# Four changes at once in a feed-forward layer by a seven-product scheme: other PSUM banks for the turned gates, down products with the weights' remainders last, one weight sum moved from a transfer to VectorE, and a new order on three engines

## The reference

```
def swiglu(x, wg, wu, wd):
    return (jax.nn.silu(x @ wg) * (x @ wu)) @ wd

h = rms_norm(x, g_ffn_pre[i])
gu = h @ w_gate_up[i]
f = (jax.nn.silu(gu[..., :D_FF]) * gu[..., D_FF:]) @ w_down[i]
x = x + rms_norm(f, g_ffn_post[i])
```

## Time and profile before

| | us |
|---|---|
| median of 3 runs | 1564.68 |
| lowest and highest | 1564.57, 1565.01 |
| the profiled execution | 1565.01 |
| its span in the profile | 1563.2 |
| TensorE matmuls busy in it | 1540.2 |
| VectorE busy | 1314.4 |
| ScalarE busy | 1019.2 |
| GpSimd busy | 155.2 |

### The profile page before, as it was taken

How to read it: one execution, slowest core, us unless ns; L and a number is a source line. 1 busy time by engine, 2 the same in 40 slices (tenths; PEclk the granted TensorE clock), 3 DMA queues, 4 the chain that set the end, 5 groups by cost and what they waited for, 6 DMA issues and landing times.

```text
span 1563.2 us, 20989 instructions
## 1 busy us (share of the span) xinstructions
PE 1540.2 (99%) x8060; PEld 1257.7 (80%) x8060; DVE 1314.4 (84%) x1420; ACT 1019.2 (65%) x1400; POOL 155.2 (10%) x232
## 2 busy tenths in 40 slices
PE   9999999999999999999999999999999999999998
PEld 8778878877888888888877888888878887788886
DVE  6869998787999989998658699988999766789996
ACT  7756776675676666666558467665766556656674
POOL 1001000040100010002030000000000203000000
PEclk9999999999999999999999999999999999999999
DMA  8338887623978868899540488977798652077992
GB/s 294 135 107 257 229 258 240 202 82 111 303 219 243 268 203 241 255 291 246 178 135 2 148 237 240 292 209 263 216 278 259 202 187 82 1 269 214 281 261 79
DMA packets 154611, 321.17 MB, mean 205 GB/s; under 512 B 5736, under 2 KB 50016, under 8 KB 151440
## 3 DMA queue, kind: packets, MB, share of 16 engines
q1 hardware_dynamic: 135408, 261.87, 48.3%
q0 software_dynamic: 18672, 57.42, 18.8%
q10 hardware_dynamic: 432, 0.53, 0.1%
HBM read 293.59 MB, written 1.05 MB: 188 GB/s over the span
## 4 chain that ended last, share of the span: by engine, by line
PE 86%; DVE 7%; DMA 3%; ACT 3%; issue 1%; SPq 0%; POOL 0%; POOLq 0%; DVEq 0%; ACTq 0%
PE pair L2893 9%; PE pair L2894 9%; PE pair L2897 9%; PE bank L2680 8%; PE bank L2682 7%; PE bank L2681 7%; PE pair L2804 7%; PE bank L2774 6%; PE pair L2808 4%; PE bank L2747 3%; PE pair L3168 2%; PE bank L3219 1%; DVE w_lo L1688 1%; PE bank L3189 1%; PE pair L2951 1%
## 5 line engine op out<-in xcount | busy, mean ns | idle before, releaser
L1052 ACT ACTIVATE w_hi<-raw 128x2048 fp32r<-128x2048 f32 (+2 forms) x171 | 325.0, 1904 | 155.9 <-DVE raw L1855 52.3
L1688 DVE TENSOR_TENSOR w_lo<-raw,w_hi 128x2048 fp32r<-128x2048 f32 (+2 forms) x167 | 378.9, 2273 | 51.0 <-ACT w_hi L1052 50.4
L1688 DVE TENSOR_TENSOR w_lo<-fold_raw,w_hi 128x2048 fp32r<-128x2048 f32 x144 | 329.4, 2288 | 28.7 <-ACT w_hi L1052 26.3
L1052 ACT ACTIVATE w_hi<-fold_raw 128x2048 fp32r<-128x2048 f32 x144 | 275.9, 1916 | 80.9 <-PE bank L2682 32.6
L2680 PE MATMUL bank<-w_hi,hid_hi 128*128 128x512 f32 x528 | 206.8, 392 | 0.3 <-DVE hid_lo L1814 0.2
L2682 PE MATMUL bank<-w_lo,hid_hi 128*128 128x512 f32 x528 | 205.8, 390 | 0.0
L2681 PE MATMUL bank<-w_hi,hid_lo 128*128 128x512 f32 x528 | 205.6, 389 | 0.0
L2893 PE MATMUL pair<-w_hi,xs_hi 128*128 128x512 f32 x384 | 154.2, 401 | 0.0
L2894 PE MATMUL pair<-w_hi,xs_lo 128*128 128x512 f32 x384 | 150.3, 391 | 0.0
L2804 PE MATMUL pair<-xt,w_hi 128*128 128x512 f32 x528 | 129.0, 394 | 0.1
L2893 PE MATMUL pair<-w_hi,xt 128*128 128x512 f32 x288 | 115.5, 401 | 1.1 <-DVE hid_lo L1915 1.1
(11 more groups left out here) (356 smaller groups left out, 2676.2 us busy)
## 6 DMA issues: line engine op xcount, KB each, us to landing
raw<-in_ffn_wd SPq DMA_DIRECT2D x44, 1024.0 KB, 9.2
fold_raw<-in_w_gate_up SPq DMA_DIRECT2D x32, 1024.0 KB, 7.5
fold_raw<-in_ffn_wg SPq DMA_DIRECT2D x32, 1024.0 KB, 6.5
fold_raw<-in_ffn_wu SPq DMA_DIRECT2D x32, 1024.0 KB, 7.3
fold_raw<-fold_raw POOLq DMA_DIRECT2D x24, 1024.0 KB, 7.2
raw<-in_w_down SPq DMA_DIRECT2D x22, 1024.0 KB, 8.5
raw<-in_w_in SPq DMA_DIRECT2D x21, 1024.0 KB, 6.3
fold_raw<-in_ffn_wu POOLq DMA_DIRECT2D x16, 1024.0 KB, 11.2
```

The lines of the kernel that those rows point to most:

```text
L1052: act.activation(w_hi[u % RING][:, 0:filled(u)], raw_of(u)[:, 0:filled(u)], ACT.Copy)\
L1688: dve.tensor_tensor(w_lo[s][:, 0:filled(u)], raw_of(u)[:, 0:filled(u)], w_hi[s][:, 0:filled(u)].bitcast(F32), ALU.subtract)\
```

## The change

- `turn_fold` writes banks 2 and 3. `fold_hidden` and `fold_rest` read there. The waits of the products follow: first and second wait for the readers of banks 0 and 1, fifth for `fold_rest(k, 0)`, fourth for `fold_rest(k, 1)`. TensorE takes first and second ahead of fifth.
- `down_inner` (groups 1 to 7, and 9 but in FFN 1) and `down_half` issue all rounded-by-rounded matmuls of their places, then all with the hidden values' remainder, then all with the weights' remainder, and wait for `hidden_lo` and `lo_ready` only ahead of the second and the third set.
- `add_to_lower` goes. VectorE makes the sum (`four_sum`), and `SUM_STEP` counts it as a VectorE step.
- The unit numbers of a fold, and the lists of SP, ScalarE and VectorE get a new order.

```diff
 FOLD_AT = ((7, 8, 9, 10, 11, 12, 14),
-           (17, 18, 16, 19, 20, 21, 23),
-           (26, 27, 25, 28, 29, 30, 32),
-           (35, 36, 34, 37, 38, 39, 41))
+           (16, 17, 18, 19, 20, 21, 23),
+           (25, 26, 27, 28, 29, 30, 32),
+           (34, 35, 36, 37, 38, 39, 41))
-SUM_STEP = (1, 16, 1, 16)
+SUM_STEP = (1, 16, 1, 1)
...
 SP
                 load_right(0)
+                load_down(2)
                 load_down(1)
-                load_down(2)
...
+                load_down(3)
                 load_down(4)
-                load_down(3)
+                load_left(2)
                 load_upper(2)
-                load_left(2)
...
                 load_left(3)
+                load_lower(3)
                 load_right(3)
-                load_lower(3)
...
 GpSimd
-                pool.wait_ge(fold_made[THREE_SUM], fold_index(f, k) + 1)
-                pool.wait_ge(lo_ready, ffns[f][0] + FOLD_AT[k][1] + 1)
-                pool.dma_start(quarters(LOWER), quarters(LEFT), accum_op=ALU.add)\
-                    .then_inc(fold_made[FOUR_SUM], 16)
...
 ScalarE
-                    act.activation(hid_hi[g % 2][:, :], bank[b], ACT.Copy).then_inc(hidden_hi, 1)
+                    act.activation(hid_hi[g % 2][:, :], bank[2 + b], ACT.Copy).then_inc(hidden_hi, 1)
...
+                first_out(1)
+                quarter_rounded(1, 4)
                 fifth_out(1)
-                quarter_rounded(1, 4)
-                first_out(1)
                 sum_rounded(1, 5)
+                second_out(1)
                 down_rounded(3)
-                second_out(1)
                 sum_rounded(1, 6)
...
 VectorE
+                def four_sum(k):
+                    landed(k, LOWER)
+                    dve.wait_ge(fold_made[THREE_SUM], fold_index(f, k) + 1)
+                    dve.wait_ge(lo_ready, u0 + FOLD_AT[k][1] + 1)
+                    dve.tensor_tensor(fold_raw[LOWER][:, :], fold_raw[LEFT][:, :], fold_raw[LOWER][:, :], ALU.add)\
+                       .then_inc(fold_made[FOUR_SUM], 1)
...
```

```diff
 TensorE
                 def first_product(k):
...
-                        pe.wait_ge(hidden_lo, hidden_base + FOLD_GROUPS[k - 1][0] + 1)
+                        pe.wait_ge(third_copied, fold_index(f, k))
...
                 def second_product(k):
-                        pe.wait_ge(hidden_lo, hidden_base + FOLD_GROUPS[k - 1][1] + 1)
+                        pe.wait_ge(fold_gate[0], fold_index(f, k))
...
                 def fifth_product(k):
...
-                        pe.wait_ge(fold_up[0], fold_index(f, k))
-                        pe.wait_ge(fold_gate[1], fold_index(f, k))
+                        pe.wait_ge(hidden_lo, hidden_base + FOLD_GROUPS[k - 1][0] + 1)
...
                 def fourth_product(k):
+                        pe.wait_ge(hidden_lo, hidden_base + FOLD_GROUPS[k - 1][1] + 1)
...
+                def down_terms(u, g, places):
+                    pe.wait_ge(hi_ready, u + 1)
+                    pe.wait_ge(hidden_hi, hidden_base + g + 1)
+                    for m, t, b in places:
+                        pe.matmul(ACC[2 * t + b][:, :], hid_hi[p][:, SEQ * m + P * t:SEQ * m + P * (t + 1)],
+                                  w_hi[s][:, D * m + 512 * b:D * m + 512 * (b + 1)], start=False, stop=False)
+                    pe.wait_ge(hidden_lo, hidden_base + g + 1)
+                    for m, t, b in places:
...
+                    pe.wait_ge(lo_ready, u + 1)
+                    for m, t, b in places:
...
+                def down_inner(g):
+                    down_terms(u0 + DOWN_AT[g], g, [(m, t, b) for m in range(2) for t in range(NT) for b in range(2)])\
+                        .then_inc(unit_used, 1)
...
                 turn_fold(0)
-                fifth_product(1)
                 first_product(1)
                 second_product(1)
+                fifth_product(1)
                 sixth_product(1)
                 third_product(1)
                 seventh_product(1)
-                down(3)
+                down_inner(3)
                 fourth_product(1)
-                down(4)
+                down_inner(4)
                 turn_fold(1)
...
                 if f == 1:
                     down_quarters(((u0 + DOWN_AT[9], 9, 1), (u0 + DOWN_AT[10], 10, 0)), ("ffn1", 0))
                 else:
-                    down(9)
+                    down_inner(9)
                     down(10)
```

More of the change, by code:

```diff
@@ L1914, in fold_rest @@
                     dve.wait_ge(hidden_hi, hidden_base + g + 1)
[L1915 removed]
+                    dve.tensor_tensor(hid_lo[g % 2][:, :], bank[2 + b], hid_hi[g % 2][:, :].bitcast(F32), ALU.subtract)\
                        .then_inc(hidden_lo, 1)
@@ L1920, in ffn @@
                 add_cross(0)
+                row_sums()
                 split_lo(u0 + GATE_AT[1])
@@ L1973, in ffn @@
                 split_lo(u0 + FOLD_AT[1][6])
+                fold_multiply(1, 0)
                 split_lo(u0 + DOWN_AT[4])
                 upper_sum(2)
+                second_gate(1)
                 second_up(1)
-                fold_multiply(1, 0)
-                second_gate(1)
-                split_lo(u0 + FOLD_AT[2][2])
-                fold_multiply(1, 1)
-                split_lo(u0 + FOLD_AT[2][0])
-                three_sum(2)
-                fold_rest(1, 0)
-                split_lo(u0 + FOLD_AT[2][1])
-                fold_rest(1, 1)
+                split_lo(u0 + FOLD_AT[2][0])
+                fold_multiply(1, 1)
+                split_lo(u0 + FOLD_AT[2][1])
+                fold_rest(1, 0)
+                three_sum(2)
+                split_lo(u0 + FOLD_AT[2][2])
                 split_lo(u0 + FOLD_AT[2][3])
@@ L2950, in turn_fold @@
                             first = SEQ * (j % 2) + P * t
-                            last = pe.transpose(bank[j // 2][:, first:first + P], hid[t][:, P * j:P * (j + 1)], ident)
+                            last = pe.transpose(bank[2 + j // 2][:, first:first + P], hid[t][:, P * j:P * (j + 1)], ident)
                     last.then_inc(fold_turned, 1)
@@ L2957, in down_half @@
                     s = u % RING
-                    if half == 0:
-                        pe.wait_ge(lo_ready, u + 1)
-                        pe.wait_ge(hidden_lo, hidden_base + g + 1)
-                    for t in range(NT):
-                        for m in range(2):
-                            lo = SEQ * m + P * t
-                            last = three(ACC[2 * t + half][:, :], hid_hi[p][:, lo:lo + P],
-                                         hid_lo[p][:, lo:lo + P],
-                                         w_hi[s][:, D * m + 512 * half:D * m + 512 * (half + 1)],
-                                         w_lo[s][:, D * m + 512 * half:D * m + 512 * (half + 1)], False, False)
+                    last = down_terms(u, g, [(m, t, half) for m in range(2) for t in range(NT)])
                     if half:
                         last.then_inc(unit_used, 1)
+                def down_terms(u, g, places):
+                    s, p = u % RING, g % 2
+                    pe.wait_ge(hi_ready, u + 1)
[5 more added lines that the diff above has]
+                    for m, t, b in places:
+                        pe.matmul(ACC[2 * t + b][:, :], hid_lo[p][:, SEQ * m + P * t:SEQ * m + P * (t + 1)],
+                                  w_hi[s][:, D * m + 512 * b:D * m + 512 * (b + 1)], start=False, stop=False)
+                    pe.wait_ge(lo_ready, u + 1)
+                    for m, t, b in places:
+                        last = pe.matmul(ACC[2 * t + b][:, :], hid_hi[p][:, SEQ * m + P * t:SEQ * m + P * (t + 1)],
+                                         w_lo[s][:, D * m + 512 * b:D * m + 512 * (b + 1)], start=False, stop=False)
+                    return last
+                def down_inner(g):
+                    down_terms(u0 + DOWN_AT[g], g, [(m, t, b) for m in range(2) for t in range(NT) for b in range(2)])\
+                        .then_inc(unit_used, 1)
                 def down(g):
@@ L3062, in ffn @@
                 seventh_product(2)
-                down(5)
+                down_inner(5)
                 fourth_product(2)
-                down(6)
+                down_inner(6)
                 turn_fold(2)
-                fifth_product(3)
                 first_product(3)
                 second_product(3)
+                fifth_product(3)
                 sixth_product(3)
@@ L3072, in ffn @@
                 seventh_product(3)
-                down(7)
+                down_inner(7)
                 fourth_product(3)
```

153 lines of the change are left out of this document (77 added, 76 removed).

## The result

| | us |
|---|---|
| changed kernel, median of 8 runs | 1569.32 (1568.70 to 1569.68) |
| kernel before, 8 runs beside them | 1564.87 (1563.82 to 1565.40) |
| ratio | 1.0025, 95% interval 1.0015 to 1.0034 (the quotient of the two medians is 1.0028) |
| profiled execution; its span | 1569.21; 1567.4 |

The change made the kernel 4.5 us slower. The forecast was 2.7 us faster. The time lies inside the whole range (1557.5 to 1571), above that of the main case (1559.5 to 1565), and on the other side of the time before. All comparisons are between undisturbed executions; one of experiment 9, the profiled one, took twice and one of experiment 10 four times as long as the others, and both are left out.

A forecast was written before the change was run, and what follows sets the result against it. TensorE was taken as the bound, with VectorE nearly as full in the fold windows. The terms -4.5 - 1.5 + 2.0 + 1.1 = -2.9 us, off the median 1564.7, gave 1561.8, stated as 1562.0 us, range 1557.5 to 1571.

The forecast's parts named there:

- main case: Whole kernel: the summed terms hold, 1562.0 us, range 1559.5 to 1565, chance 0.49.
- the sum on VectorE: Fourth sum moved to VectorE: delays the fifth product in fold 1 through fold_rest(0, 0), +2.0 us over all FFNs.
- the ends of FFN 2 and 4: Behind the last folds there: FFNs other than FFN 1 use the new down form and don't wait, no cost.
- The banks and `second_out`: Turned gates in banks 2 and 3, -4.5 us; second_out ahead of down_rounded ends the up_sum waits, -1.5 us.
- the first down product: FFN 3 and 5: it waited for hidden_rest(0), which comes earlier, so some 0.2 us is gained.
- The walk: VectorE's list in FFN 1 from hidden_rest(0): fold_rest(0, 0) ends at 468.6, fourth product 0.8 us later.
- The moved quarter loads each still have 8 us to land: Quarter loads moved in the lists: each still has 8 us to land.
- The end of FFN 1: down_quarters waits for its remainder, whose split now stands behind fold_rest(3, 0): +1.1 us, once.
- The down order: Down products with remainders last: nothing by itself, a cushion for the sum worth 1.1 us in each FFN.
- A: Rival, fold windows: VectorE becomes the bound, each full window needs 31.9 us; 1572, or 1588 at worst; chance 0.20.
- C: Rival: gains and losses meet, late VectorE takes back in the next product what the banks give; 1564.7; chance 0.13.
- B: Rival: no stall in fold 1, 1558.4; shared weights shorten the down pitch, 1554.5; chance 0.18, 0.03 of it shared weights.

The follow-up runs named there:

- experiment 9: Changed kernel with the fourth sum again a transfer from SBUF to SBUF instead of on VectorE; 1564.63 us, 0.9998 of the kernel before.
- experiment 10: Changed kernel with the fourth sum as a transfer and row_sums back behind add_up(0); 1559.57 us, 0.9966 of the kernel before.
- experiment 5: Changed kernel with row_sums back behind add_up(0) on VectorE; 1571.67 us, 1.0037 of the kernel before.
- experiment 8: Changed kernel with the old down products, weight remainders needed at the start, in place of down_inner; 1610.58 us, 1.0287 of the kernel before.
- experiment 12: Changed kernel with the fourth sum as a transfer and the old order of the down products; 1579.47 us, 1.0095 of the kernel before.
- Experiment 1: Changed kernel with VectorE's remainder of down 7 ahead of four_sum(3) in fold 3; 1566.74 us, 1.0011 of the kernel before.
- experiment 3: Changed kernel with GpSimd's 16 small loads in FFN 2 and 4 released by the end of down 7, 5.5 us later; 1578.98 us, 1.0093.
- experiment 2: Changed kernel with ScalarE rounding the turned bank (fold_hidden(3, 0)) ahead of the last wd unit (down_rounded(10)); 1572.06 us, 1.0049 of the kernel before.
- experiment 4: Changed kernel with VectorE's split of the next part's first unit behind three residual additions in FFN 2 and 4; 1572.58 us, 1.0054.
- experiment 6: Changed kernel with row_sums behind add_up(0) and fold_rest(0, 0) ahead of fold 1's third split; 1568.70 us, 1.0021 of the kernel before.
- experiment 7: Changed kernel with VectorE's remainder of down 9 ahead of fold_rest(3, 0); 1570.04 us, 1.0030 of the kernel before.

## Why the prediction was wrong

The sum said -2.9 us and +4.5 was measured. The gains came nearly as predicted. Two terms failed: the sum on VectorE, whose price of +2.0 lay at another wait and came to +5.0 in four parts (less 1.2 in the other two), and the ends of FFN 2 and 4, put at 0 and measured at +5.5. Experiments 9, 10, 5 and the changed kernel make a table of four, in us:

| | row_sums ahead of add_up(0) | row_sums behind it |
|---|---|---|
| sum on VectorE | 1569.32 (the change) | 1571.67 |
| sum as a transfer | 1564.63 | 1559.57 |

From 1564.6 the other parts give -5.1; `row_sums` early costs 5.1 where VectorE has the time; the sum costs 4.7 in the list as changed and 12.1 with `row_sums` late. These are differences within one table, so that they add up to the change (-5.1 + 5.1 + 4.7) is no proof of them. The two parts are not independent: `row_sums` early costs 5.1 us beside the transfer and gains 2.4 with the sum on VectorE. Some 1.7 us of the 12.1 are the half clock at the end of FFN 2 in experiment 5 (an estimate, 0.34 of 5 us).

**The banks and `second_out`, predicted -6.0: right in size.** No run puts either back alone, so their shares, 4.5 and 1.5, are not shown apart, nor apart from the orders of loads and splits. Without the sum and with `row_sums` back the folds give 6.7 us, and of the waits of the earlier trace rows the one for `up_sum` is gone and the one for `hid_lo` is 1.7 us, 6 times. Folds 2 and 3 take 31.09 and 28.28 us where about 31.0 and 28.3 were predicted. The first stages of FFN 3 and 5 became 0.5 to 0.7 us shorter (predicted 0.2 each for the first down product, and 0.2 for what comes behind). The first part of that is seen: before, the first down product started 0.50 and 0.40 us behind its predecessor, 0.23 us of it idle in FFN 3:

```profile
911.28 0.47 PE L2680 MATMUL bank<-w_hi,hid_hi 128*128 128x512 f32 x1 [0.23 <-DVE hid_lo L1814]
```

That wait is gone in the changed kernel and in experiments 8 and 12, where the old down order then loses 0.8 us at downs 1 and 2 of the same stage. So it is not the down order that gives it; `hidden_rest(0)`, which comes earlier in all of these, likely does.

**The sum on VectorE, predicted +2.0: the step that failed first.** The walk put `fold_rest(0, 0)` of FFN 1 at 468.6 and the product's readiness at 467.65. Changed kernel, VectorE and TensorE:

```profile
467.71 0.69 DVE L1914 TENSOR_TENSOR hid_lo<-pair,hid_hi 128x512 fp32r<-128x512 f32 x1
```

```profile
467.64 1.07 PE L2900 MATMUL pair<-w_lo,xt 128*128 128x512 f32 x4
468.55 0.41 PE L2896 MATMUL pair<-w_hi,xs_hi 128*128 128x512 f32 x1
```

The rest ends at 468.40, so the walk was good to 0.2 us, in part by luck: large operations one behind the other take 2.20 us in the changed kernel and not 2.285 (0.7 us over eight), and a wait of 0.62 us for ScalarE at 427.41, which the walk did not have, made up for it. But the product starts at 468.55 right behind its predecessor, because TensorE was already 0.9 us late: it had lost 1.3 at `up(1)`. I began the walk at `hidden_rest(0)` and had not asked who reads what `row_sums` now stood in front of. In FFN 0 to 2 and 4 that wait costs 1.4, 1.4, 1.3 and 0.9 to 1.0 us (predicted, for the fifth product: 0.8, 0.8, 0.8 and 0.4). VectorE was busy for 1357.4 us in all where 1369 was predicted: its records overlap, and 24 more of 2.29 us add less than 55.

**"The moved quarter loads each still have 8 us to land", "the other FFNs use the new form there and don't wait": the costlier failure, +5.5 us for a predicted 0.** The first sentence asked for the loads that were moved in SP's list. The load that hurt wasn't moved; VectorE's extra 2.3 us in fold 3 delayed the split that frees its tile. Experiment 1 shows it; experiment 3 shows the other half, the loads of GpSimd's queue that stand on no row that I had read. The transfer engines' share in the first window of FFN 1 did fall, from 0.92 to 0.75, and says nothing about these 10 us. The Trainium skill (DMA: Bandwidth & Descriptors, "Queues, rings and completion order") says that each transfer engine takes packets in turn from the queues with work; the trace agrees in so far as the last `wd` load, which takes 4.9 us ahead of GpSimd's loads, takes 10.5 and 11.1 beside them, but no row here shows the turns. Nor does a run tell whether the number of GpSimd's loads or their 2.1 MB does it.

**The end of FFN 1, predicted +1.1: right.** `fold_rest(3, 0)` starts at 554.39, the splits behind it at 554.99, and the quarters wait for the first (the earlier trace rows have them at 556.10):

```profile
554.39 0.69 DVE L1914 TENSOR_TENSOR hid_lo<-pair,hid_hi 128x512 fp32r<-128x512 f32 x1 [1.74 <-ACT hid_hi L1282]
554.99 4.49 DVE L1679 TENSOR_TENSOR w_lo<-raw,w_hi 128x2048 fp32r<-128x2048 f32 x2
```

```profile
557.33 0.50 PE L2683 MATMUL bank<-w_hi,hid_hi 128*128 128x512 f32 x1 [0.91 <-DVE w_lo L1679]
```

**The down order, predicted 0 by itself and 1.1 us in each FFN as a cushion (6.6): mis-sized.** Taken out, it costs 41.3 us with the sum on VectorE and 14.8 without. I had priced one late remainder in one fold; in experiment 8 the wait recurs at 28 places. The likely reason, argued and not isolated by a run: a late TensorE also gives `unit_used` late, the ring of three makes ScalarE and then VectorE wait for it, and the lead doesn't come back. ScalarE's waits for a down product are 126.1 us (44 times) in experiment 8 and 85.3 (40 times) in the changed kernel.

**The rivals.** A (VectorE becomes the bound, 1572) has the right sign and nearly the time, by another way: no fold of the changed kernel is longer than before, and the second window holds 30.15 us of VectorE where A wants 31.9. Where the down order is old (experiment 8) it is as A describes. C would have the folds unchanged, and they are 6.4 us shorter. B asked for a lower pitch of the down products; theirs is still 0.2267 us (23 steps in 5.21 us in FFN 1), with a weight load for each matmul.

**Still open.** A load of the first `w_in` unit ahead of GpSimd's loads was not tried, and the banks, `second_out` and the orders of loads were not put back alone. What decides whether the clock falls behind a stall of some 2 us is not known from these runs; it is part of the profiled executions of experiments 2, 4, 5, 6 and 7, and so most likely of their medians.

## What to carry to other kernels

When an instruction is moved up in a list, ask for the reader of everything that it now stands in front of, from the first place on where the lists differ; and when an engine gets more work, follow the buffers that it frees to the transfers that wait for them, and see what else is on the transfer engines by then. A stall that is removed shows its worth only if the next one isn't just behind it: of the six moves here that each took a stall away (experiments 1 to 5 and 7) one made the kernel faster and three made it slower by 2.7 us or more. Before a change of many parts is judged, put parts back alone and in pairs: here the transfer alone gave 4.7 us back, `row_sums` alone made it 2.4 slower, and both together gave 9.8.

## What the runs showed that I had not expected

- 16 loads of GpSimd, 2.1 MB together and issued over 9.9 us, make the last `wd` load of 1 MB take 10.5 and 11.1 us in place of 4.9, and the first `w_in` load behind it 12.8 and 13.7 in place of 8.2 and 7.8. In FFN 4 of the kernel before, TensorE didn't wait behind the turning for all that.
- After 5.99 us without work TensorE ran at the lower level (1.2 of 2.4 GHz): the mean granted clock is 0.66 in the 10 us that hold the end of the stall, 1.00 before and behind, and the records of its matmuls start 0.43 us apart in place of 0.2267. So that stall cost more than its length.
- At the ends of FFN 2 and 4 the clock also fell at shorter stalls, of 1.95 to 4.5 us (experiments 2, 4, 5, 6 and 7). It did not behind those of 1.22 and 1.81 us in the changed kernel's FFN 4, nor behind one of 2.49 us in experiment 4. Each such fall cost 1.6 us or more (an estimate from the windows above), more than the wait at `up(1)` costs in one part.
